# Expert weights, router weights, normed rows and gated product in partition-major order of features

## The reference, cut to what matters

```
h = rms_norm(x, norm2_g)                       # 1032 x 1024
g = h @ w_router_group + b ; e = h @ w_router_expert + b
group = argmax(g) ; two experts of that group by top_k(e)
for each chosen pair (token, expert):
    y = (silu(h @ w_gate[e]) * (h @ w_up[e])) @ w_down[e]
x = x + sum of the token's two y, weighted
out = rms_norm(x, norm_f_g)
```

## Time and profile before

| | |
|---|---|
| median of three executions | 1852.25 us (1849.06 to 1852.56) |
| profiled execution, span from first to last instruction | 1856.1 us |
| its own time outside of the span | not listed |
| TensorE matmul busy | 1671.0 us |
| TensorE weight loads busy | 1482.8 us |
| VectorE busy | 1031.1 us |
| ScalarE busy | 836.9 us |
| GpSimd busy | 272.3 us |
| DMA, mean over the span | 164 GB/s |
| DMA in the slices of the expert stage | 296 to 340 GB/s |

### The profile page before, as it was taken

One profiled execution on the slowest core, in us unless ns is written; L12 is line 12 of the kernel. 1 busy time (PEld: TensorE's weight loads), 2 busy tenths in 40 slices (PEclk: granted clock), 3 DMA queues, 4 the chain that ended last, 5 costly groups with the idle time before them and its releaser, 6 DMA issues.

```text
span 1856.1 us, 26370 instructions
## 1 busy us (share of the span) xinstructions
PE 1671.0 (90%) x9491; PEld 1482.8 (80%) x9491; DVE 1031.1 (56%) x1780; ACT 836.9 (45%) x1210; POOL 272.3 (15%) x287
## 2 busy tenths in 40 slices
PE   5999999999999999999999968888899888888860
PEld 4899899999999999999988846777677776777750
DVE  5321566566664321132244557777777867777747
ACT  5000455555554301131122216666667766676633
POOL 1100000000000000000001121332223322233200
PEclk9999999999999999999999978999999989999985
DMA  5332111111113011231134138898999989898807
GB/s 152 93 102 76 49 41 41 45 45 45 45 34 106 24 46 48 71 121 45 45 129 158 69 137 306 318 327 317 323 325 331 340 296 326 321 328 316 316 25 274
DMA packets 187891, 304.15 MB, mean 164 GB/s; under 512 B 29364, under 2 KB 91032, under 8 KB 187552
## 3 DMA queue, kind: packets, MB, share of 16 engines
q1 hardware_dynamic: 172688, 267.27, 41.4%
q0 software_dynamic: 15152, 36.18, 5.4%
HBM read 286.97 MB, written 35.19 MB: 174 GB/s over the span
## 4 chain that ended last, share of the span: by engine, by line
PE 71%; DMA 11%; POOL 8%; issue 3%; DVE 3%; ACT 2%; POOLq 1%; ACTq 0%; SPq 0%; DVEq 0%
PE bank L1019 10%; DMA xg<-normed_rows,gcol 10%; PE bank L690 9%; PE bank L692 8%; PE bank L691 8%; PE bank L835 6%; PE bank L836 5%; PE bank L837 5%; POOL idle_out L616 4%; POOL gcol L611 3%; PE bank L998 2%; PE bank L784 2%; PE bank L965 2%; PE bank L967 2%; PE bank L969 2%
## 5 line engine op out<-in xcount | busy, mean ns | idle before, releaser
L1824 DVE TENSOR_TENSOR e_lo<-e_raw,e_hi 128x2048 fp32r<-128x2048 f32 x192 | 434.2, 2289 | 142.3 <-ACT e_hi L1317 142.2
L1317 ACT ACTIVATE e_hi<-e_raw 128x2048 fp32r<-128x2048 f32 x192 | 364.9, 1920 | 99.3 <-PE bank L1019 62.0
L1007 PE MATMUL bank<-e_hi,xT_hi 128*128 128x512 f32 x512 | 205.8, 402 | 5.0 <-DVE xT_lo L1829 5.0
L690 PE MATMUL bank<-h_hi,w_hi 128*128 128x344 f32 x624 | 202.6, 325 | 1.1 <-DVE h_lo L1435 1.1
L1009 PE MATMUL bank<-e_hi,xT_lo 128*128 128x512 f32 x512 | 203.2, 397 | 0.0
L1008 PE MATMUL bank<-e_lo,xT_hi 128*128 128x512 f32 x512 | 202.4, 395 | 0.0
L1101 ACT ACTIVATE w_hi<-w_raw 128x1024 fp32r<-128x1024 f32 x68 | 71.6, 1053 | 284.4 <-PE bank L692 252.7
L691 PE MATMUL bank<-h_lo,w_hi 128*128 128x344 f32 x624 | 199.8, 320 | 0.0
L692 PE MATMUL bank<-h_hi,w_lo 128*128 128x344 f32 x624 | 199.7, 320 | 0.0
L835 PE MATMUL bank<-h_hi,w_hi 128*128 128x344 f32 x576 | 196.6, 341 | 2.0 <-DVE w_lo L1416 2.0
L836 PE MATMUL bank<-h_lo,w_hi 128*128 128x344 f32 x576 | 184.1, 320 | 0.0
(11 more groups left out here) (318 smaller groups left out, 3251.1 us busy)
## 6 DMA issues: line engine op xcount, KB each, us to landing
e_raw<-in_w_e_gate_dram SPq DMA_DIRECT2D x64, 1024.0 KB, 6.6
e_raw<-in_w_e_up_dram SPq DMA_DIRECT2D x64, 1024.0 KB, 7.3
e_raw<-in_w_e_down_dram SPq DMA_DIRECT2D x64, 1024.0 KB, 4.8
w_raw<-in_w_in_dram SPq DMA_DIRECT2D x104, 256.0 KB, 3.2
f_y<-expert_rows SPq DMA_DIRECT2D x16, 512.0 KB, 8.7
a_spill<-y_sb POOLq DMA_DIRECT2D x8, 516.0 KB, 2.9
a_raw<-a_spill SPq DMA_DIRECT2D x2, 2064.0 KB, 9.6
x_tok<-in_x_prompt_dram SPq DMA_DIRECT2D x4, 1024.0 KB, 10.6
```

The source lines that it names most:

```text
L690: pe.matmul(out, wh, xh, start=i == 0, stop=False)
L1007: pe.matmul(out, xT_hi[:, par, kk, :], wh, start=kk == 0, stop=False)
L1317: A.activation(e_hi[:, slot % 4, :], e_raw[slot][:, :], ACT.Copy).then_inc(e_hi_done, 1)
L1824: V.tensor_tensor(e_lo[slot][:, :], e_raw[slot][:, :], e_hi[:, slot % 4, :].bitcast(F32), ALU.subtract).then_inc(e_lo_done, 1)
```

## The change

The feature that stands in partition p, part k is now 8 p + k (4 p + k for the inner 512 features of an expert), in the gate, up, down and router weights, and the rows that meet them are put in the same order: the normed rows when they are written by second_norm, the gated product when it is written by activate, in both places by a VectorE instruction that was there before and now writes with a step of 128 elements. Transposes, matmuls, splits, the gather and all semaphores stay as they are. A chunk of expert weights is then one run of 8 KB for each partition, 16 KB apart.

```
-                w = (w_e_gate if c < 2 else w_e_up)[0].rearrange("e (k p) f -> e p k f", p=P)
+                w = (w_e_gate if c < 2 else w_e_up)[0].rearrange("e (p k) f -> e p k f", p=P)
                 return w, e, slice(4 * (c % 2), 4 * (c % 2) + 4)
-            return w_e_down[0].rearrange("e (k p) f -> e p k f", p=P), e - 1, slice(2 * (c % 2), 2 * (c % 2) + 2)
+            return w_e_down[0].rearrange("e (p k) f -> e p k f", p=P), e - 1, slice(2 * (c % 2), 2 * (c % 2) + 2)
...
-            pool.dma_start(wr[:, :, 0:NG], w_router_group[0].rearrange("(k p) g -> p k g", p=P)).then_inc(router_loaded, 16)
-            pool.dma_start(wr[:, :, NG:NG + NE], w_router_expert[0].rearrange("(k p) g -> p k g", p=P)).then_inc(router_loaded, 16)
+            pool.dma_start(wr[:, :, 0:NG], w_router_group[0].rearrange("(p k) g -> p k g", p=P)).then_inc(router_loaded, 16)
+            pool.dma_start(wr[:, :, NG:NG + NE], w_router_expert[0].rearrange("(p k) g -> p k g", p=P)).then_inc(router_loaded, 16)
...
-                src = x2[0:rows, bass.ds(n, 1), :].rearrange("p a d -> p (a d)")
-                V.scalar_tensor_tensor(xn[0:rows, :], src, rms[0:rows, 1:2], g2b[0:rows, :], ALU.mult, ALU.mult).then_inc(xn_done, 1)
+                src = x2[0:rows, bass.ds(n, 1), :].rearrange("t a (p k) -> t (a p) k", k=KT)
+                V.scalar_tensor_tensor(xn[0:rows, :].rearrange("t (k p) -> t p k", p=P), src, rms[0:rows, 1:2],
+                                       g2b[0:rows, :].rearrange("t (p k) -> t p k", k=KT), ALU.mult, ALU.mult).then_inc(xn_done, 1)
...
-                V.tensor_tensor(act_sb[:, :], sg[:, :], bank[1][:, :], ALU.mult).then_inc(act_done, 1)
+                V.tensor_tensor(act_sb[:, :].rearrange("t (k p) -> t p k", p=P), sg[:, :].rearrange("t (p k) -> t p k", k=4),
+                                bank[1][:, :].rearrange("t (p k) -> t p k", k=4), ALU.mult).then_inc(act_done, 1)
```

More of the change, by code:

```diff
@@ L493, in _ @@
                         for dst, w in ((v_gate, w_e_gate), (v_up, w_e_up), (v_down, w_e_down)):
-                            sp.dma_start(dst[:, :, :], w[0][bass.ds(ex, 1)].rearrange("e (k p) f -> p (e k) f", p=P)).then_inc(v_loaded, 16)
+                            sp.dma_start(dst[:, :, :], w[0][bass.ds(ex, 1)].rearrange("e (p k) f -> p (e k) f", p=P)).then_inc(v_loaded, 16)
             sp.wait_ge(rows_written, 1)
@@ L1886, in _ @@
                         dve.wait_ge(v_silu, i + 1)
-                        V.tensor_tensor(act_sb[:, :], sg[:, :], bank[1][:, :], ALU.mult).then_inc(v_act, 1)
+                        V.tensor_tensor(act_sb[:, :].rearrange("t (k p) -> t p k", p=P), sg[:, :].rearrange("t (p k) -> t p k", k=4),
+                                bank[1][:, :].rearrange("t (p k) -> t p k", k=4), ALU.mult).then_inc(v_act, 1)
                         dve.wait_ge(v_apsum, i + 1)
```

## The result

The changed kernel is slower: 1898.76 us (1897.66 to 1903.76, 4 runs) against 1850.65 us for the kernel before in runs on the same chip, ratio 1.026, 95% interval 1.0225 to 1.0294. The forecast was 1829 us and its range ended at 1890.

The account below looks back on a forecast made before the run. The prediction took the expert stage to be bound by a ring through the gather, not by late loads. Its terms, -14.5 - 8.5 + 0 = -23 us off the 1852.3 median, gave 1829 us, range 1800 to 1890.

Parts of the forecast that it names:

- What bounds the stage: Expert stage: loads are not late; TensorE waits for the gather, 69.5 us in 29 waits.
- the ring: Expert stage: down product, store, scatter issue, gcol, idle_out, gather, turn, down product again; a round takes 20.5 us.
- Part 1: Gate and up chunks in 8 KB runs: queue ahead of the gather empties 0.5 us sooner, 14.5 us less over 29 gathers.
- The turns rival: Engines take turns by runs, so 8 KB weight runs delay the gather: middle 1883 us, worst 1914; slower case 0.30.
- the two rows that spoke for it: Third gather near 4 KB-run down chunks (7.7 us) and a 12 KB load behind x_tok loads (5.0), cited for turns.
- the 12 KB load: Load issued right behind the first x_tok loads (4 KB runs); took 5.0 us, cited as evidence for turns.
- Part 2: TensorE's clock: ten slow down products after longer waits cost 17 us; shorter waits remove half, 8.5 us less.
- Parts 3 and 5: Down chunks land before the gather's issue: zero; router weights, loaded once on GpSimd's queue: 0, at most 1 us.
- Part 4: VectorE's stepped writes of xn and act_sb: at most twice as long, taken as 0; last xn 0 to 1.3 us.
- the far third of the slower case: The part of the slower case (0.30) above 1890 us, left out of the 8-in-10 range.

Follow-up runs that it names:

- after_late: The changed kernel (8 KB runs) with each expert's first up chunk issued some 1.9 us later; 0.9928 of the kernel before.
- down_only: The kernel before with the new order for the down weights and gated product alone; ratio 0.9986 to the kernel before.
- step_only: The kernel before with only VectorE's two instructions changed to write with a step of 128 elements; ratio 1.0008 to the kernel before.
- new_cut: The changed kernel with each chunk taking every second row of a partition, so runs of 2 and 4 KB with gaps; 1.02 of the kernel before.
- new_split: The changed kernel, same 8 KB DRAM reads, but written in SBUF as four pieces of 2 KB, 4 KB apart; 0.9911 of the kernel before.

## Why the prediction was wrong

- *What bounds the stage* was right: the gather in the ring, not the loads. SP still waits for TensorE (206 us behind gate and up products).
- *Part 1 failed, and with it the sign.* It held that quicker loads empty the queue ahead of the gather 0.5 us sooner, and that this gives -14.5 us. The loads did get quicker (427 against 397 GB/s, gate 0.2 us sooner), and the gather still got longer, by 0.9 us on the mean of 29: +25.9 us. The step took the queue as one line served by bytes, in which the gather waits for the gate chunk and then gets its share. It is not: with the same bytes and addresses, 2 KB runs give a gather of 5.7, 4 KB 6.4 and 8 KB 7.3 us. The turns rival had this right, and named the chunk, the first up chunk: issued 1.9 us later, it leaves a gather of 5.8 us (after_late). Its price, +1.1 us and 32 us at worst, was near the measured 0.9 and 25.9; the 30 us that it put on the clock beside it were 14.2. I gave it 0.30 because the two rows that spoke for it had 3 to 4 MB of backlog, and counted it half when placing the range. For the 12 KB load, one of the two, the quoted rows have no time without load to compare with. My reading that the rate does not rise beyond runs of 4 KB was wrong as well: 415 GB/s at 4 KB, 427 at 8 KB over one stretch; by itself it would have made the forecast lower still.
- *Part 2 had the right mechanism and the wrong sign,* since it hung on shorter waits. A slow down product costs 1.3 us over the 5.5 of the others before and 1.4 after; seven more came instead of five fewer: +10.5 us. With the turns (+3.7) it is +14.2 us against the -8.5 forecast.
- *Parts 3 and 5* held: down_only is 0.9986, and the first gather after stage D comes within 1.2 us of before.
- *Part 4* held: the writes took 1.5 and 1.6 times as long, within the doubling allowed, and step_only is 1.0008. The 1.2 us by which the first gather comes later is the one visible piece, against 0 taken and 1.3 as bound.
- *The range* ended at 1890 because the far third of the slower case was left out; the rival's full price was computed to 1914 in the same text, and the measured 1899 lies between the two. A mechanism without a limit on one side should have held the upper end.

The cost of each packet, which I took from the Trainium skill's page "DMA: Bandwidth & Descriptors", section "Why small descriptors are slow", does not decide here. My estimate from its figure is a rate lower by 3.4% at 2 KB and by 7.5% at 1 KB than at 8 KB. The measured rates are lower by 7.5% (395 against 427 GB/s) and 17% (353), the same direction and over twice the size.

The Trainium skill's page "DMA: Bandwidth & Descriptors" says in its section "Queues, rings and completion order" that each engine drains a packet of descriptors from one queue row before it goes to the next. The runs agree with that in the sign and, from 2 to 8 KB, in the dose. How many runs go in a turn they do not show. Nor do they exclude another reason why long runs get ahead: the gather's issue keeps GpSimd for 1.06 us, the up chunk is issued just behind it, and with runs of 8 KB SP issues it in 0.33 us in place of 0.37. Runs of 4 KB are issued in 0.37 us too and have a longer gather than runs of 2 KB (6.4 against 5.7 us, on different chips), which speaks against it. Which of the two transfers reaches the engines first was not tried. That run length is the cause is shown, by what path is argued.

## What to carry to other kernels

When a small transfer that is waited for shares the DMA engines with a bulk stream that is early anyway, longer runs in the stream can raise its rate and still lengthen the small transfer, as here; look first at who waits for what, and size the runs for the one that is waited for. Try more than one length: here 2 KB was best, and both 8 KB and 1 KB lost. A load that need not be early can be issued a little after the transfer that must be quick: here 1.9 us cured the whole loss. A control that changes run length by leaving gaps in DRAM (new_cut) changed how late each load lands as well; cutting the runs on the SBUF side (new_split) hardly did, 5.3 to 7.1 us against 5.0 to 6.9 in the changed kernel.

## What the runs showed of the hardware that I had not expected

- Reading every second 2 KB of a stretch (new_cut, gate and up chunks) makes a 1 MB load land 8.6 to 8.9 us after issue, against 6.4 to 7.1 for runs of the same length without gaps (new_split), though both move the same with a full queue (397 and 395 GB/s).
- A run that is contiguous on one side only is still cut: the same 8 KB of DRAM written to SBUF in four pieces counts as four packets (new_split), as four pieces of DRAM written side by side do (the kernel before).
- 2 KB runs with all 1 MB of a chunk in one stretch are 1.1% faster as a kernel than 2 KB runs whose partitions lie 16 KB apart. Why is open: the version also writes xn and the gated product in two instructions each, though step_only makes it unlikely that VectorE matters.
- In the changed kernel gathers whose up chunk is issued 1.06 us behind them take 0.9 us more on the mean than those with 1.26 us. That this shift is the reason is not shown.
